# Holding back the last two experts' down weights until the eighth pass's rows have landed

## The chip, the cores and the metric

The kernel runs on one core of one Trainium2 chip. The metric is the device time of one execution in microseconds (us), taken as the median of several runs; smaller is better.

## The reference, cut to what matters

One decoder layer runs over 536 tokens of width 1024: 16 meta tokens, 512 prompt tokens and 8 sample tokens. First comes a mixer (RWKV-7 time mixing and retention, merged by gates, then an output projection). Then comes the part that the change touches, a mixture of 16 experts of which every token uses two, and a final RMSNorm:

```python
x = x + m
x = x + hier_moe(rmsnorm(x, p['norm2_g']), p)
...
h = (jax.nn.silu(jnp.einsum('btd,edf->btef', u, p['expert_w_gate']))
     * jnp.einsum('btd,edf->btef', u, p['expert_w_up']))
h = h * combine[..., None].astype(h.dtype)
return jnp.einsum('btef,efd->btd', h, p['expert_w_down'])
...
y_prompt = rmsnorm(xp[:, N_META:], final_norm_g)
```

All in float32. `combine` is zero except at a token's two experts (top 2 of 4 within the best of 4 groups). A gate and up weight of one expert is 2 MB together (`w_gu`), its down weight 1 MB (`w_dn`).

## The kernel before, in words

The mixer fills the first 640 us and is not touched. After it, the residual rows `x2` lie in DRAM (`x2_dram`, shown as x_rows) and the normed rows in another DRAM tensor (u_rows). Every expert has 96 slots for tokens (`CAP`), so 16 experts make 1536 slots, worked through as 12 passes of 128 slots (`NPASS`), numbered 0 to 11. A pass covers parts of two experts. Slots without a token carry an index out of bounds, and their rows are skipped by the indirect DMAs.

For a pass `e` the work goes round all engines:

- GpSimd (POOL) gathers its 128 rows from u_rows (L1069).
- TensorE (PE) transposes them (`to_channels`, L2589), multiplies them by the gate and up weights (`gate_up`, L2609), transposes the hidden rows (`hidden_in`, L2618) and multiplies them by the down weights (`down`, L2643; for the last pass L2636).
- ScalarE (ACT) does the sigmoid (L2678), copies the transposed hidden rows (`hidden_out`, L2684), and for passes 0 to 7 scales the product rows (`rows_out`, L2693).
- VectorE (DVE) forms the gated product and scales the transposed inputs (L2765).
- For passes 0 to 7 POOL then scatters the rows onto `x2_dram` with an add in the DMA (L2551). Each such scatter raises the semaphore `q_yd[e % 2]` by 16. `ADDS` holds the full counts: 80 for the even passes 0, 2, 4, 6, 8, and 64 for the odd passes 1, 3, 5, 7. So `q_yd[1]` is at 64 once the scatter of pass 7, the eighth, has landed.
- Pass 8 (`SUMS`) is different: its residual rows are gathered ahead (L2557), DVE adds the product to them (L2819), and POOL scatters the sums without an add (L2546).
- Passes 9, 10 and 11 (the three `LATE` ones) never go back to `x2_dram`. When all scatters have landed, POOL gathers their residual rows (L2564), DVE adds their products (L2811, and L2844 in two halves for pass 11), and the rows are normed and scattered straight into the output (L2576).

The order on TensorE near the end is: gate_up(9), down(8), to_channels(11), gate_up(10), hidden_in(9), gate_up(11), hidden_in(10), down(9), hidden_in(11), down(10), down(11).

The final norm of the other tokens runs on tiles of 128 rows, 0 to 4. When both `q_yd` semaphores are full (L2510), SyncE (SP) loads the five tiles from `x2_dram` into SBUF (L2515). ACT squares and sums a tile (L2706) and takes the root (L2715), DVE takes the reciprocal (L2803) and multiplies (L2805), and SP stores the tile (L2520). ACT's instruction stream interleaves these with the last passes: tiles 0 and 1 are squared before the sigmoid and the hidden copy that passes 10 and 11 need, tile 2 after them. So the first two tiles gate the last passes too.

The weights: SP issues all weight loads into six buffers (`NWE`), in one queue, in the order of the loop at L2503. In step `i` it waits until the buffer's gate and up part is free and issues `load_gu(i)` (L957), then waits until the down part of buffer `i - 1` is free and issues `load_dn(i - 1)` (L960). The experts are numbered 0 to 15 in order of use; `load_dn(14)` is issued in step 15 and `load_dn(15)` in step 16. `load_gu(15)` comes before `load_dn(14)`. `down(10)` is the first to use down weight 14 and `down(11)` the first to use down weight 15.

Of the kernel before, what the change touches and what calls it, by code (L numbers as in the profile page):

```python
# [39 lines left out]
NE, NG, EPG, FF = 16, 4, 4, 256  # L40
# [21 lines left out]
def expert_at(i):  # L62

    return EPG * (i % NG) + i // NG
# [379 lines left out]
def hybrid_step(nc, I, O):  # L444

    with ExitStack() as ctx:
# [3 lines left out]
        def sem(name):  # L450
            assert name not in sem_names
            sem_names.add(name)
            return E(nc.semaphore(name))
# [320 lines left out]
        def un_ps(kind, n):  # L774
            p0, p1, c0, c1 = UNITS[n]
            return job_ps((kind, n), (p1 - p0) * (c1 - c0)).rearrange("t (p k) -> t p k", p=p1 - p0)

        NLEV = [sum(1 for b in LEVELS[1:] if b < w) for _, w in CHUNKS]

        def tiles_of(c):  # L780
# [149 lines left out]
        q_yd = [sem(f"q_yd{i}") for i in range(2)]  # L930
# [19 lines left out]
        def rows_of(t):  # L950
            return LASTT if t == TT - 1 else P
# [4 lines left out]
        def load_gu(eng, i):  # L956
            eng.dma_start(we[i % NWE][:, 0:4096], I["w_gu"][expert_at(i)]).then_inc(s_we[i % NWE], 16)  # L957

        def load_dn(eng, i):
            eng.dma_start(we[i % NWE][:, 4096:6144], I["w_dn"][expert_at(i)]).then_inc(s_wd[i % NWE], 16)  # L960

        def load_expert(eng, i):
            load_gu(eng, i)
            load_dn(eng, i)
# [316 lines left out]
        def _(pe):  # L1281
# [8 lines left out]
            def first_pair(step, part):  # L1290

                _, m, hf = step
                ps = job_ps(step) if part else open_job(step)
                i = (m - RET0) // RH
                edges = FIRST[(m, hf)]
                if hf == 0 and part == 0:
                    pe.wait_ge(s_w[i], 16)
                for k in range(edges[part], edges[part + 1]):
                    if (m, hf, k) == (RET0, 0, KD // 2):
                        pe.wait_ge(s_rets, 16)  # L1300
                    if i == 0:
                        pe.wait_ge(s_xg, KD * hf + k + 1)
                    last = mm(ps, wt[:, i, k, :], xg[:, k, cols(hf)], start=(k == 0), stop=(k == KD - 1))  # L1303
                if part == len(edges) - 2:
                    last.then_inc(s_job, 1)

            def whole(step, part):

                _, m, hf = step
                ps = job_ps(step) if part else open_job(step)  # L1310
                side = FILL[0].index(m)
                if part == 0:
                    pe.wait_ge(s_w[2], 32)
                for k in range(2 * part, 2 * part + 2):
                    last = mm(ps, fill_in(0)[side][:, k // 2, k % 2, :], u[:, k, cols(hf)], start=(k == 0), stop=(k == KD - 1))  # L1315
                if part == PARTS["j_proj"] - 1:
                    last.then_inc(s_job, 1)
# [1130 lines left out]
        ADDS = [16 * len(range(q, NPASS - LATE, 2)) for q in range(2)]  # L2448
# [13 lines left out]
        def last_pass(i):  # L2462
            return (CAP * (i + 1) - 1) // P
# [22 lines left out]
        with nc.Fori(0, rounds) as r:  # L2486
            def at_least(eng, s, per, n):
                assert n > 0
                eng.wait_ge(s, r * per + n)

            with nc.Block(no_gpsimd_drain=True) as block:
                @block.sync
                def _(sp):
                    sp.wait_ge(d_x, 3)
                    sp.wait_ge(d_lt, 3)
                    for q in range(2):
                        at_least(sp, q_g[q], EVERY, 16)
                    load_dn(sp, 3)
                    sp.dma_start(O["retp"], ret_st).then_inc(z_out[1], 16)
                    load_expert(sp, 4)  # L2500
                    sp.wait_ge(d_x2w, 16 * TT)
                    load_expert(sp, 5)
                    for i in range(NWE, NE + 1):  # L2503
                        if i < NE:
                            at_least(sp, q_gu, NPASS, last_pass(i - NWE) + 1)
                            load_gu(sp, i)
                        if i > NWE:
                            at_least(sp, q_dn, DOWNS, last_pass(i - 1 - NWE) + 1)
                            load_dn(sp, i - 1)
                    for q in range(2):  # L2510
                        at_least(sp, q_yd[q], ADDS[q], ADDS[q])
                        sp.nop(nofuse=True)
                    for t in range(TT):
                        n = rows_of(t)
                        sp.dma_start(xf[0:n, t, :], x2_dram[t * P:t * P + n, :]).then_inc(z_x[t], 16)  # L2515
                    for t in range(TT):
                        at_least(sp, z_y, TT + LATE, t + 1)
                        sp.nop(nofuse=True)
                        n = rows_of(t)
                        sp.dma_start(O["y"][t * P:t * P + n, :], xf[0:n, t, :]).then_inc(z_out[t % 2], 16)  # L2520
                    for j in range(LATE):
                        at_least(sp, z_late[j], 16, 16)
                    sp.nop(nofuse=True)
                    at_least(sp, z_out[0], 48, 48)
                    at_least(sp, z_out[1], 48, 48)
                    sp.nop(nofuse=True)
# [430 lines left out]
```

## Time and profile before

| | |
|---|---|
| median of 3 runs | 811.1 us (810.11 to 812.12) |
| the profiled execution's own time | 811.99 us |
| its span | 810.5 us |
| PE busy | 778.4 us (96%) |
| DVE, ACT, POOL busy | 432.5, 210.8, 39.2 us |
| bytes moved by DMA | 127.19 MB |
| mean granted TensorE clock | 0.987 of full speed |

The span runs from the first to the last instruction that the profiler recorded. The 1.5 us between it and the profiled execution's time lie around it. Times in the rows below count from the span's start. A DMA instruction's row tells when it was issued and how long the issuing engine was held; when its data landed is a time of its own, given from the start of the issue. A row of the chain names what the end of the program was waiting for at that moment.

### The profile page before, as it was taken

The numbers are of one execution on the slowest core, as the hardware profiler recorded it, in microseconds if no ns is written. First come the engines' busy times: TensorE is split into PE (matmuls) and PEld (weight loads), VectorE is DVE, ScalarE is ACT, GpSimd is POOL, SyncE is SP. The second block draws the span as 40 slices with busy tenths as digits, with TensorE's granted clock in tenths as the row PEclk, the third lists the DMA queues.
The fourth block names the chain that finished last, engine by engine and source line by source line (L and its number), as shares of the span: only waits on it lengthen the run. The fifth ranks groups of instructions, "written<-read, shape, count | busy, mean of one in ns | idle before, by whom it ended". The sixth has DMA issues, their size and how long they took to land.

```text
span 810.5 us, 19993 instructions
## 1 busy us (share of the span) xinstructions
PE 778.4 (96%) x8538; PEld 537.0 (66%) x8538; DVE 432.5 (53%) x855; ACT 210.8 (26%) x497; POOL 39.2 (5%) x50
## 2 busy tenths in 40 slices
PE   7999999999999999999999999999999889999993
PEld 5877777787767877777777877767788633333331
DVE  5965667688768565657666555346204431101135
ACT  4122222254523312211212232220022411111134
POOL 0000000000000000000000000000000011222111
PEclk9999999999999999999999999999999889999997
DMA  9541432432212101201230112064935689999964
GB/s 328 194 157 52 134 106 77 159 105 73 83 53 80 53 28 56 68 15 52 74 121 28 34 50 80 3 234 197 357 131 199 240 304 401 392 404 387 379 225 164
DMA packets 36678, 127.19 MB, mean 157 GB/s; under 512 B 5827, under 2 KB 16099, under 8 KB 31728
## 3 DMA queue, kind: packets, MB, share of 16 engines
q1 hardware_dynamic: 32560, 115.78, 38.3%
q0 software_dynamic: 4032, 10.15, 4.2%
q8 instruction: 68, 1.11, 0.6%
q14 instruction: 18, 0.15, 0.1%
HBM read 106.83 MB, written 18.68 MB: 155 GB/s over the span
## 4 chain that ended last, share of the span: by engine, by line
PE 89%; DVE 5%; DMA 3%; issue 2%; ACT 1%; SPq 0%; POOL 0%; DVEq 0%; POOLq 0%; ACTq 0%
PE psum L1370 23%; PE psum L1351 12%; PE psum L1703 9%; PE psum L2609 9%; PE psum L2643 4%; PE psum L1328 4%; DVE arena L2050 2%; PE psum L1315 2%; PE psum L1303 2%; PE psum L1571 2%; PE psum L1659 1%; PE psum L1584 1%; PE psum L2589 1%; PE psum L1468 1%; PE psum L1480 1%
## 5 line engine op out<-in xcount | busy, mean ns | idle before, releaser
L2050 DVE TENSOR_TENSOR arena<-arena 128x268 f32<-128x268 f32 (+10 forms) x322 | 175.3, 544 | 48.0 <-ACT arena L1802 28.8
L1370 PE MATMUL psum<-arena 128*128 128x268 f32 x784 | 189.5, 393 | 0.0
L1370 PEld LDWEIGHTS psum<-arena 128*128 128x128 f32 x784 | 145.1, 189 | 37.8 <-issue 11.6
L1802 ACT ACTIVATE arena<-psum 128x268 f32<-128x268 f32 (+7 forms) x215 | 85.5, 405 | 276.9 <-PE psum L1370 143.9
L2050 DVE TENSOR_TENSOR arena<-psum,arena 128x256 f32<-128x256 f32 (+5 forms) x170 | 71.7, 426 | 80.2 <-PE psum L1584 21.8
L1351 PE MATMUL psum<-arena 128*128 128x268 f32 x392 | 105.0, 402 | 0.0
L1703 PE MATMUL psum<-arena 128*128 128x268 f32 x384 | 91.0, 391 | 1.6 <-DVE arena L2050 1.2
L2609 PE MATMUL psum<-arena 128*32 128x512 f32 (+1 forms) x640 | 85.7, 597 | 0.5 <-DVE arena L2765 0.3
L1351 PEld LDWEIGHTS psum<-arena 128*128 128x128 f32 x392 | 69.7, 189 | 20.4 <-issue 6.3
L1703 PEld LDWEIGHTS psum<-arena 128*128 128x128 f32 x384 | 71.1, 189 | 17.7 <-issue 3.3
L2765 DVE TENSOR_TENSOR arena<-psum,arena 128x256 f32<-128x256 f32 (+2 forms) x38 | 24.3, 663 | 100.7 <-ACT arena L2678 90.8
L1802 ACT ACTIVATE arena<-arena 128x268 f32<-128x268 f32 (+10 forms) x121 | 49.4, 454 | 105.6 <-PE psum L1715 59.0
L2609 PEld LDWEIGHTS psum<-arena 128*32 128x32 f32 (+1 forms) x640 | 25.2, 115 | 57.4 <-issue 56.8
L2053 DVE SCALAR_TENSOR_TENSOR arena<-arena 128x536 f32<-128x536 f32 (+7 forms) x71 | 41.6, 585 | 12.7 <-DMA arena<-arena 5.8
L2643 PE MATMUL psum<-arena 128*32 128x512 f32 (+1 forms) x288 | 40.2, 596 | 0.0
L2053 DVE SCALAR_TENSOR_TENSOR arena<-psum,arena 128x268 f32<-128x268 f32 (+2 forms) x23 | 10.3, 450 | 47.7 <-PE psum L1703 39.6
L1328 PE MATMUL psum<-arena 128*128 128x268 f32 x128 | 34.4, 401 | 0.0
L2053 DVE SCALAR_TENSOR_TENSOR arena<-arena,psum 128x268 f32<-128x268 f32 (+1 forms) x36 | 18.8, 522 | 19.7 <-PE psum L1703 12.2
L1274 POOL MEMSET arena<- 64x256 f32 (+1 forms) x18 | 5.5, 312 | 489.9 <-PE psum L1370 266.2
L2050 DVE TENSOR_TENSOR arena<-arena,psum 128x268 f32<-128x268 f32 (+3 forms) x35 | 18.2, 520 | 18.8 <-PE psum L1351 14.2
L1328 PEld LDWEIGHTS psum<-arena 128*128 128x128 f32 x128 | 22.7, 189 | 6.5 <-issue 1.9
L2643 PEld LDWEIGHTS psum<-arena 128*32 128x32 f32 (+1 forms) x288 | 10.8, 115 | 21.3 <-issue 21.3
(210 smaller groups left out, 696.0 us busy)
## 6 DMA issues: line engine op xcount, KB each, us to landing
arena<-in_w_gu SPq DMA_DIRECT2D x16, 2048.0 KB, 21.7
arena<-in_w_in SPq DMA_DIRECT2D x45, 512.0 KB, 4.4
arena<-in_w_dn SPq DMA_DIRECT2D x16, 1024.0 KB, 20.0
arena<-in_w_out SPq DMA_DIRECT2D x2, 2048.0 KB, 14.1
arena<-arena SPq DMA_DIRECT2D x5, 536.0 KB, 5.9
arena<-in_x SPq DMA_DIRECT2D x8, 268.0 KB, 5.5
arena<-arena SPq DMA_DIRECT2D x16, 134.0 KB, 4.5
arena<-in_x SPq DMA_DIRECT2D x1, 2144.0 KB, 14.5
```

The costliest lines, as they stand in the source:

```text
L1303: last = mm(ps, wt[:, i, k, :], xg[:, k, cols(hf)], start=(k == 0), stop=(k == KD - 1))
L1315: last = mm(ps, fill_in(0)[side][:, k // 2, k % 2, :], u[:, k, cols(hf)], start=(k == 0), stop=(k == KD - 1))
L1328: last = mm(ps, bb_tile(m)[:, k, :], ret_o[:, k, cols(hf)], start=(k == 0), stop=(k == NP - 1))
L1351: last = mm(ps, w[:, k // 2, k % 2, :], x[:, k, :], start=(k == 0 and i in (0, 1, 3)), stop=(k == KD // 2 - 1), skip_group_check=i not in ...
L1370: last = mm(ps, w[:, k, :], x[:, k, :], start=(k == 0 and i in (0, 1, 3)), stop=(k == KD // 2 - 1), skip_group_check=i not in (0, 1, 3))
L1703: last = mm(ps, w[:, k, :], x[:, k, cols(hf)], start=(k == 0), stop=(k == nk - 1))
L1802: run(nc.scalar.activation(out, in_, fn, **kw), s)
L2050: run(v.tensor_tensor(out, a, b, op), s)
L2053: run(v.scalar_tensor_tensor(out, a, sc_, b, op0, op1), s)
L2609: last = mm(bank(2 + i % 2)[part], ue[:, i % 2, k, part], w_gu[x % NWE][:, k, :], start=(k == 0), stop=(k == KD - 1))
L2643: last = mm(bank(down_bank(e) + q)[part], hht(e)[:, f, part], w_dn[x % NWE][:, f, 512 * q:512 * q + 512], start=(f == 0), stop=(f == 1))
L2765: v.tensor_tensor(out, x, y, op).then_inc(s, 1)
```

## The change

SyncE gets one more wait, ahead of the issue of down weight 14. With NE = 16 the condition holds in step 15 only. Down weight 15, the next instruction but one in the same stream, thereby also comes after it.

```diff
@@ -2506,6 +2506,8 @@
                             load_gu(sp, i)
                         if i > NWE:
                             at_least(sp, q_dn, DOWNS, last_pass(i - 1 - NWE) + 1)
+                            if i - 1 == NE - 2:
+                                at_least(sp, q_yd[1], ADDS[1], ADDS[1])
                             load_dn(sp, i - 1)
                     for q in range(2):
                         at_least(sp, q_yd[q], ADDS[q], ADDS[q])
```

## Rows read from the trace of the kernel before

**Rows 1.** The page: shares of the chain that ended last, by engine.
```profile
PE 89%; DVE 5%; DMA 3%; issue 2%; ACT 1%; SPq 0%; POOL 0%; DVEq 0%; POOLq 0%; ACTq 0%
```

**Rows 2.** The chain that ended last, 764 to 811: start us, us, what.
```profile
766.33 3.62 PE psum L2643 x32
769.97 1.30 DVE arena L2819
...
772.10 7.71 DMA x_rows<-arena,ids
...
780.00 4.47 DMA arena<-x_rows
...
793.71 1.28 DVE arena L2811
```

**Rows 3.** Instructions in order of time on SP: start, us, line; x2 is two.
```profile
741.56 0.33 SPq L957 DMA_DIRECT2D arena<-in_w_gu  x1
746.40 12.02 SPq L960 DMA_DIRECT2D arena<-in_w_dn  x2
...
758.10 0.33 SPq L960 DMA_DIRECT2D arena<-in_w_dn  x1
```

**Rows 4.** Instructions in order of time on POOL, in brackets the idle time before.
```profile
760.14 1.60 POOL L2551 DMA_INDIRECT x_rows<-arena,ids  x1 [3.86 <-ACT arena L2693]
772.10 1.00 POOL L2546 DMA_INDIRECT x_rows<-arena,ids  x1 [10.37 <-DVE arena L2819]
780.76 1.03 POOL L2564 DMA_INDIRECT arena<-x_rows,ids  x1 [7.66 <-DMA x_rows<-arena,ids]
```

**Rows 5.** DMA issues one at a time, from 741.56, 746.40, 758.10, 760.14: us to landing last.
```profile
arena<-in_w_gu SPq DMA_DIRECT2D x1, 2048.0 KB, 32.2
...
arena<-in_w_dn SPq DMA_DIRECT2D x1, 1024.0 KB, 30.1
...
arena<-in_w_dn SPq DMA_DIRECT2D x1, 1024.0 KB, 21.5
...
x_rows<-arena,ids POOLq DMA_INDIRECT x1, 15.0
```

**Rows 6.** DMA issues: output scatters; all down-weight loads; third tile load; last late gather.
```profile
out_y<-arena,ids POOLq DMA_INDIRECT x3, 3.3
...
DMA to landing us min/median/max: 4.8/20.0/30.9
...
arena<-x_rows SPq DMA_DIRECT2D x1, 512.0 KB, 7.4
...
arena<-x_rows,ids POOLq DMA_INDIRECT x1, 8.4
```

**Rows 7.** Busy time by stretch; the last two columns are DMA share and GB/s.
```profile
764.00:768.00 4.00, 4.00 (x39) 1.77 (x34) 2.00 (x3) 0.73 (x2) 0.00 (x0) 1.00 1.01 381
768.00:772.00 4.00, 3.66 (x32) 1.59 (x26) 1.91 (x2) 0.00 (x0) 0.00 (x0) 1.00 0.78 255
772.00:776.00 4.00, 4.00 (x20) 1.29 (x18) 0.60 (x1) 0.00 (x0) 1.00 (x1) 1.00 0.41 156
776.00:780.00 4.00, 4.00 (x29) 1.21 (x29) 0.85 (x2) 1.57 (x3) 0.00 (x0) 1.00 0.13 55
```

**Rows 8.** DMA queues from 782 to 785: packets, MB, share of 16 engines.
```profile
q1 hardware_dynamic: 265, 0.96, 81.3%
q0 software_dynamic: 84, 0.21, 22.3%
```

**Rows 9.** Instructions in order of time on PE and ACT, 770 to 796.
```profile
770.25 1.09 PE L2589 MATMUL psum<-arena 128*128 128x128 f32 x8 [0.34 <-DMA arena<-u_rows,ids]
...
790.47 3.66 PE L2643 MATMUL psum<-arena 128*64 128x512 f32 x16
795.13 3.64 PE L2636 MATMUL psum<-arena 128*32 128x512 f32 x32 [1.00 <-DVE arena L2811]
...
784.49 1.06 ACT L2706 ACTIVATE arena<-arena 128x1024 f32<-128x1024 f32 x1 [3.82 <-DMA arena<-x_rows]
...
785.87 1.04 ACT L2706 ACTIVATE arena<-arena 128x1024 f32<-128x1024 f32 x1
```

## The prediction

> **What bounds the kernel now.** I read the page first, then the chain of waits from 764 us on, then the DMA issues one by one, and last the DMA share by stretch. The page says that the chain is 89% TensorE [rows 1], and up to 770 us there is nothing for this change to shorten: the chain is matmuls back to back. At the end it is different. From 769.97 the chain goes through L2819 on VectorE, then through the last scatter (772.10, 7.71 us), then through the load of row tile 0 (issued 780.00, 4.47 us), and from there through ScalarE and VectorE to the end [rows 2]. TensorE has idle time in this part (1.00 us ahead of the last pass's down product [rows 9]), so 12.2 us of pure DMA time stand on the path. If these get shorter or longer, the end moves with them.
>
> Why does the scatter of pass 8 take 7.71 us, when the output scatters at the very end land 3.3 us after their issue [rows 6]? Look at what is in flight. Gate/up weight 15 was issued at 741.56 and took 32.2 us, so it landed at 773.8. Down weight 14, issued at 746.40, took 30.1 and landed at 776.5. Down weight 15, issued at 758.10, took 21.5 and landed at 779.6 [rows 3, 5]. The three come in the order of issue, and the last comes 0.2 us before the scatter (779.8). The scatter of pass 7, issued at 760.14, took 15.0 us and landed at 775.1 [rows 4, 5]. In the same stretches the DMA share falls from 1.01 to 0.78, 0.41 and 0.13 [rows 7]: most of the 16 DMA engines have drained, and a few still work off all of their queue. Skipped rows explain that (my reading): slots without a token are always the last ones of an expert's 96, so some engines get more real rows than others. A transfer has landed only when the last engine has done its part, so the laggards set all these times.
>
> **The change, part by part.**
>
> Issue. Down weight 14 moves from 746.40 to the landing of the scatter of pass 7, and down weight 15 from 758.10 to right after it. Behind the waiting SyncE instruction stand down weight 15, the wait for both scatter semaphores, the five tile loads and the stores. Gate/up weight 15 is ahead of it. The wait is not met already: 746.40 against 775.1. One more wait instruction costs nothing to see, SyncE is idle there.
>
> Landing of the scatter of pass 7. The laggards' queue up to gate/up weight 15 is as before, for the down weights stood behind it. The gathered input of pass 11 landed at 770.25 (TensorE waited 0.34 us for it [rows 9]) and is ahead of the scatter in POOL's queue, so the scatter used 4.9 us from 770.2 to 775.1. Up to 773.8 all is as before, 3.6 of the 4.9 us. The other 1.3 us ran beside down weight 14. POOL's queue has 22% of the engines' time when both queues are full [rows 8], so alone the rest takes 0.3 us: 774.1. One more gain is possible: while all engines are busy, each moves 381 / (16 x 1.01) = 23.6 GB/s, in the drained stretch 55 / (16 x 0.13) = 26 [rows 7]. With 2 MB fewer on the other engines the laggards could gain up to 10% over some 7 us, 0.7 us. I take a small part of it: 773.9. Bounds: 773.3 and 775.1 (no gain).
>
> Landing of the scatter of pass 8. Its issue, 772.10, hangs on TensorE and VectorE and stays. It now follows pass 7's on empty queues: 3.3 us from issue would be 775.4, but its data start only at 773.9, some 2.3 us more give 776.3; I take 776.5. Bounds 775.4 and 779.8. So the tile loads are issued at 776.7 and not at 780.00, and the late gathers at 777.4 and not at 780.76 [rows 4]. This is the gain, 3.3 us at the issue.
>
> What it triggers. The tile loads stand in SyncE's queue behind 2.1 MB of down weights that are only now on their way. The shortest landing of one down weight was 4.8 us [rows 6]; the second adds 1.05 MB at 0.39 MB per us (0.96 + 0.21 MB in 3 us [rows 8]), 2.7 us. Issued at 774.1, the pair is in at 781.6 if nothing else runs. From about 778.5 the three late gathers take 22%, 0.6 us more: 782.2. Then tile 0: 0.52 MB at 78% of 0.39 is 1.7 us, so 783.9, against 784.47 before. Tile 1 comes 1.7 us later, at 785.6; ScalarE squared it at 785.87 before [rows 9]. So of 3.3 us about 0.3 are left, and the chain behind ScalarE starts 0.3 us earlier. The 2.1 MB were moved from a time when the DMA engines ran anyway into the hole (share 0.41 and 0.13) ahead of the tile loads, and they fill that hole to the brim.
>
> Covers. Down weight 14 is first used at 790.47, down weight 15 at 795.13 [rows 9]. At 779 and 782 they have 11 and 13 us; only landing later than that would cost. Tile 2 landed 7.4 us after its issue at 780.85 (788.2) and the last late gather 8.4 after 783.41 (791.8) [rows 6]; VectorE used it at 793.71 [rows 2]. The same bytes after a shorter pause end no later: from 775 on, 2.1 MB of down weights, 2.2 of tiles and 1.1 of gathers (about 90 rows of 4 KB each) are 5.4 MB or 13.8 us, 789.
>
> **The sum.** 811.99 for the profiled execution, minus 0.3, is 811.7. That execution stood 0.9 above the median of the runs shown, so on the median 811.1 - 0.3 = 810.8. The case's own range: from 809.6 to 812.0, by the bounds of the scatter of pass 7 (-0.6 and +1.2 on the tile loads).
>
> **A rule of the Trainium skill that speaks against this.** In the stretch from 782 to 785 POOL's queue moved 0.21 MB beside 0.96 MB of SyncE's [rows 8], though its first gather started late in it. The Trainium skill, "DMA: Bandwidth & Descriptors", section "Queues, rings and completion order", says that each DMA engine goes in turn between the queues that have work, a packet at a time. Equal turns of packets of equal bytes would give the late gathers half, not 22%; what that would give is the second rival. The row speaks for less than half, but not clearly.
>
> **Rivals.**
>
> 1. The gain gets through, 809.1. The scatter of pass 7 lands at 773.3 and the down weights pass before the late gathers take much: the pair lands at 781.0, tile 0 at 782.5 and tile 1 at 783.9. ScalarE's chain starts 2.0 us earlier. For it: the 10% faster engines above, and a hole of 8 us for 5.4 us of transfer. Against it: it needs the late gathers to cost nothing beside the pair.
>
> 2. Slower, 812.7. The late gathers take half of the engines from 778.9, since they are issued early now. Then some 0.8 MB of down weights, tile 0 (0.52) and up to 1.1 MB of gathers must pass first: 2.4 / 0.39 = 6.2 us, 785.1, and 1 us to the landing, 786.1. Tile 1 follows at 787.4 against 785.87: about +1.6. This decides as soon as gathers are issued while more than half a megabyte of down weights is still out. For it: the tiles are last in their queue, and the path hangs on the first two. Against it: the 22%.
>
> 3. The change does not do what it says for the scatter, 811.6. Its semaphore comes at 775.1 as before, and the down weights (data from 776) meet pass 8's scatter on all engines. It lands near 779.8, the tile loads find the tail of the pair ahead: tile 0 at 785.0, +0.5.
>
> 4. A new stall of TensorE for a down weight, or anything larger than these: beyond 2.4 us either way.
>
> **How the numbers follow.** Forecast 0.50, rival 1 0.20, rival 2 0.14, rival 3 0.09, rival 4 0.07. 0.3% is 2.4 us, and less than that a measurement of this kernel cannot tell from no change. Forecast, rivals 2 and 3 lie inside it; rival 1 at -2.0 with its spread falls outside in about four of ten, 0.08. With 0.05 and 0.02 of rival 4: faster 0.13, same 0.80, slower 0.07. The range of 808.6 to 813.0 takes in rivals 1 and 2 with their spread.
>
> **What the changed profile would show.** SyncE's two L960 issues side by side near 774, the first after a wait for DMA on x_rows. The scatter of pass 8 in the chain at about 4.4 us and not 7.71. The load of tile 0 issued near 776.7 and taking about 7 us and not 4.47: the gain turned into queueing. DMA share near 1 from 776 on. TensorE at L2643 and L2636 without a wait for weights. The prediction is wrong if tile 0's load starts early and stays at 4 to 5 us (rival 1 or more), if the late gathers land long before tile 0 (rival 2), or if the issues stand later than 775.1.

## The result

The changed kernel is slower. Its median was 813.62 us (812.08 to 815.43, 8 runs) beside 811.89 for the kernel before on the same chip (8 runs). The ratio, which the comparison gives and which is a little off the quotient of the two medians, is 1.0026, 95% interval 1.0016 to 1.0036, so +1.3 to +2.9 us. The forecast was 810.8 (0.3 us faster) and a range of 808.6 to 813.0. The profiled execution took 812.84 us with a span of 811.3.

The changed kernel's line numbers are two higher from the change on. Its chain of waits from 760 on (start us, us, what) answers to [rows 2]:

```profile
766.54 3.62 PE psum L2645 x32
770.19 1.30 DVE arena L2821
...
772.32 3.25 DMA x_rows<-arena,ids
...
776.08 10.48 DMA arena<-x_rows
...
794.44 1.28 DVE arena L2813
```

The scatter of pass 8 takes 3.25 us and not 7.71. But the load behind it now takes 10.48 us and is tile 1's (it ends at 786.56); before it was tile 0's, 4.47 us. The two DMA steps together went from 12.2 to 13.7 us.

The instructions on SP and on POOL, in order of time, answer to [rows 3, 4]:

```profile
741.78 0.33 SPq L957 DMA_DIRECT2D arena<-in_w_gu  x1
773.71 0.96 SPq L960 DMA_DIRECT2D arena<-in_w_dn  x2
775.71 2.44 SPq L2517 DMA_DIRECT2D arena<-x_rows  x5
```

```profile
760.36 1.60 POOL L2553 DMA_INDIRECT x_rows<-arena,ids  x1 [3.86 <-ACT arena L2695]
772.32 1.00 POOL L2548 DMA_INDIRECT x_rows<-arena,ids  x1 [10.37 <-DVE arena L2821]
776.53 1.03 POOL L2566 DMA_INDIRECT arena<-x_rows,ids  x1 [3.21 <-DMA x_rows<-arena,ids]
```

Both down weights leave from 773.7 on, the tiles 4.3 us and the late gathers 4.2 us earlier than before. How long the scatters of passes 7 and 8 took to land, from the DMA issues (before: 15.0 [rows 5] and 7.71):

```profile
x_rows<-arena,ids POOLq DMA_INDIRECT x1, 13.3
...
x_rows<-arena,ids POOLq DMA_INDIRECT x1, 3.3
```

Busy time by stretch (last columns DMA share and GB/s) answers to [rows 7]. The DMA engines are partly idle from 764 to 776 and then full up to 788:

```profile
764.00:768.00 4.00, 4.00 (x40) 1.77 (x34) 2.00 (x3) 0.73 (x2) 0.00 (x0) 1.00 0.69 210
768.00:772.00 4.00, 4.00 (x33) 1.61 (x27) 1.81 (x2) 0.00 (x0) 0.00 (x0) 1.00 0.23 73
772.00:776.00 4.00, 4.00 (x22) 1.41 (x20) 0.61 (x1) 0.00 (x0) 1.00 (x1) 1.00 0.50 151
776.00:780.00 4.00, 4.00 (x30) 1.19 (x30) 0.85 (x2) 1.75 (x3) 2.86 (x3) 1.00 1.00 408
780.00:784.00 4.00, 4.00 (x40) 1.18 (x36) 0.00 (x0) 0.48 (x2) 0.17 (x1) 1.00 1.02 414
784.00:788.00 4.00, 4.00 (x38) 1.14 (x34) 1.46 (x2) 2.83 (x6) 0.00 (x0) 1.00 1.00 389
```

The two DMA queues of the changed kernel, from 778 to 781 and from 781 to 784 (packets, MB, share of 16 engines):

```profile
q1 hardware_dynamic: 187, 1.18, 94.0%
q0 software_dynamic: 13, 0.04, 3.1%
...
q1 hardware_dynamic: 189, 0.70, 57.5%
q0 software_dynamic: 188, 0.55, 45.4%
```

The upper of each pair is SyncE's queue, the lower POOL's. POOL's queue, the late gathers, has 45% in the second stretch; the forecast used 22% from [rows 8]. What ScalarE and TensorE make of it, beside [rows 9]:

```profile
784.48 1.06 ACT L2708 ACTIVATE arena<-arena 128x1024 f32<-128x1024 f32 x1 [3.99 <-DMA arena<-x_rows]
786.58 1.06 ACT L2708 ACTIVATE arena<-arena 128x1024 f32<-128x1024 f32 x1 [0.63 <-DMA arena<-x_rows]
```

```profile
785.50 0.44 PE L2620 MATMUL psum<-arena 128*128 128x128 f32 x2
790.82 0.44 PE L2620 MATMUL psum<-arena 128*128 128x128 f32 x2 [1.30 <-DVE arena L2767]
795.86 3.64 PE L2638 MATMUL psum<-arena 128*32 128x512 f32 x32 [1.01 <-DVE arena L2813]
```

ScalarE waits for tile 0 as before and then 0.63 us more for tile 1; TensorE's last stretch waits for what comes of that, and never for a weight. All behind it is 0.7 us later.

**A measure for the tail.** What lies ahead of this stretch shifts by up to 4 us from one profile to the next (the product below ends between 785.49 and 789.51), so profiles are compared here from the end of pass 11's gate/up product (the first PE row above, 785.50) to the end of the span. This tail was 810.5 - 785.69 = 24.8 us in the first profile of before and 25.8 in the changed kernel.

### The profile page after: what moved, and what is told of

It is laid out like the page before. It is cut to its first block, busy times and chain, and to the rows that moved or that the text cites. A ratio compares the mean times of both kernels' runs of the same rounds, so it can differ in the third digit from the quotient of the medians.

```text
span 811.3 us, 19993 instructions
## 1 busy us (share of the span) xinstructions
PE 778.5 (96%) x8538; PEld 536.7 (66%) x8538; DVE 432.4 (53%) x855; ACT 211.1 (26%) x497; POOL 39.2 (5%) x50
## 4 chain that ended last, share of the span: by engine, by line
PE 89%; DVE 5%; DMA 3%; issue 2%; ACT 1%; SPq 0%; POOL 0%; DVEq 0%; POOLq 0%; ACTq 0%
PE psum L1370 23%; PE psum L1351 12%; PE psum L1703 9%; PE psum L2611 9%; PE psum L2645 4%; PE psum L1328 4%; DVE arena L2050 2%; PE psum L1315 2%; PE psum L1303 2%; PE psum L1571 2%; PE psum L1659 1%; PE psum L1584 1%; DMA arena<-x_rows 1%; PE psum L2591 1%; PE psum L1468 1%
## 5 line engine op out<-in xcount | busy, mean ns | idle before, releaser
L2053 DVE SCALAR_TENSOR_TENSOR arena<-arena,psum 128x268 f32<-128x268 f32 (+1 forms) x36 | 18.8, 521 | 19.8 <-PE psum L1703 12.2
```

Of the source, the lines that this page charges most:

```text
L2053: run(v.scalar_tensor_tensor(out, a, sc_, b, op0, op1), s)
```

## The experiments

Each edit is against the kernel before unless it says otherwise. Ratios are to the kernel before on the same chip. "The tail" is the measure above, from one profile each.

**Cut down weights, with the wait.** Nearly all of down weights 14 and 15 is left out of the transfers. Edit on the changed kernel:

```diff
+            n = 6144 if i < NE - 2 else 4224
-            eng.dma_start(we[i % NWE][:, 4096:6144], I["w_dn"][expert_at(i)]).then_inc(s_wd[i % NWE], 16)
+            eng.dma_start(we[i % NWE][:, 4096:n], I["w_dn"][expert_at(i)][:, 0:n - 4096]).then_inc(s_wd[i % NWE], 16)
```

> The changed kernel, but the last two experts' down weights load only 64 of their 2048 columns (their products are then wrong); wait and order stay. Theory A (the 2.1 MB ahead of the row tiles in SyncE's queue give the scatter's gain back): the scatter of pass 8 lands 3.3 us after its issue as in the changed kernel, tile 0 lands 4.5 us after its issue near 780.2 and not at 784.5, tile 1 by 781.6, and the time falls to about 2.5 us under the kernel before (ratio 0.997), where TensorE's gate/up product of pass 11 (end near 785.6) takes over as the bound. Theory B (the wait or the late issue itself costs, or TensorE lacks the weights): tile 0 stays near 784 and the time stays 1 to 2 us over the kernel before.

Measured: 809.72 us, ratio 0.9968 (0.9955 to 0.9980), tail 808.6 - 786.62 = 22.0 us. ScalarE's first square no longer waits for a tile, and TensorE's last product waits for nothing. ScalarE, then TensorE:

```profile
781.52 1.05 ACT L2709 ACTIVATE arena<-arena 128x1024 f32<-128x1024 f32 x1
```

```profile
794.53 3.64 PE L2639 MATMUL psum<-arena 128*32 128x512 f32 x32
```

So theory A holds: with the wait in place and the bytes gone, the loss is gone, and the bytes ahead of the tiles are the cost.

**The same cut without the wait.**

> The kernel before (no extra wait), with the last two experts' down weights cut to 64 of their 2048 columns (their products are then wrong). Theory A (the wait itself costs nothing, only where the 2.1 MB stand): the same time as the run with the cut weights and the wait, 2.4 us under the kernel before (ratio 0.997), the scatter of pass 8 landing 3.3 to 3.5 us after its issue. Rival (the wait or the late issue has a cost of its own): 0.5 us or more faster than that run.

Measured: 809.69 us, ratio 0.9967 (0.9955 to 0.9980), tail 811.5 - 789.51 = 22.0 us. The same, within intervals of some 1 us either way: no cost of the wait itself can be seen, and the pair of down weights costs the kernel before 2.7 us, the changed kernel 4.8 (1.0026 - 0.9967 of 812 us).

**Only the last down weight held.** Edit on the changed kernel (down weight 14 leaves as in the kernel before):

```diff
-                            if i - 1 == NE - 2:
+                            if i - 1 == NE - 1:
```

> Only down weight 15 is held for the scatter of pass 7; down weight 14 is issued at 746.4 as before. Theory A: 1.05 MB instead of 2.1 MB stand ahead of the tiles, but the lagging DMA engines still carry down weight 14 to 776.5. The scatter of pass 7 lands at 775.1, down weight 15 is in at about 780, the scatter of pass 8 near 777.5, tile 0 lands near 783 and tile 1 near 785: the time is 0.5 to 1 us under the kernel before. Theory B (holding any weight costs in itself): between the kernel before and the changed one, about +0.9 us.

Measured: 810.86 us, ratio 0.9986 (0.9978 to 0.9995), faster than both kernels; tail 24.1. The squares of tiles 0 and 1:

```profile
782.35 1.06 ACT L2708 ACTIVATE arena<-arena 128x1024 f32<-128x1024 f32 x1 [1.61 <-DMA arena<-x_rows]
...
785.09 1.06 ACT L2708 ACTIVATE arena<-arena 128x1024 f32<-128x1024 f32 x1 [1.26 <-DMA arena<-x_rows]
```

**The same once more.**

> Down weight 15 alone held for the scatter of pass 7, once more: 1 to 1.3 us under the kernel before (ratio 0.998 to 0.999), tile 1 in ScalarE 0.4 to 0.8 us before the end of TensorE's gate/up product of pass 11. Rival (the first time was chance): ratio 1.000.

Measured: 810.75 us, ratio 0.9981 (0.9972 to 0.9990), tail 23.5. ScalarE started on tile 1 at 784.81, 1.7 us ahead of the end of gate/up (786.51), more than the 0.4 to 0.8 expected. The scatter of pass 8 took 5.73 us here and 3.85 in the run before. The chain ends over the last late gather (issued 781.71, 11.39 us), for which VectorE waits 0.47 us, and no longer over a tile.

**Late gathers held back, in the changed kernel.** POOL waits for tile 0 ahead of them:

```diff
+                    then(z_x[0], 16, 16)
                     for j in range(LATE):
                         e = FIRST_LATE + j
                         pool.indirect_dma_start(late[:, j, :], None, x2_dram,
```

> The changed kernel, and POOL issues the three late gathers only when tile 0 has landed. Theory A with the gathers' share as the term that was too small: tiles 0 and 1 land about 1.1 and 1.5 us earlier than in the changed kernel, at 783.4 and 785.1, tile 1 before ScalarE wants it; but the gathers land some 4 us later than in the changed kernel, the last near 792.5, about when VectorE wants it, so that the time is within 0.5 us of the kernel before (1 to 2 us under the changed kernel). Rival (the down weights alone fill the time, the gathers take nothing that matters): tile 0 stays at 784.5, tile 1 at 786.6, and the time is that of the changed kernel or up to 1 us over it.

Measured: 813.08 us, ratio 1.0026 (1.0010 to 1.0041). In the profile tiles 0 and 1 come 2.0 and 1.4 us earlier than in the changed kernel:

```profile
782.49 1.06 ACT L2709 ACTIVATE arena<-arena 128x1024 f32<-128x1024 f32 x1 [1.92 <-DMA arena<-x_rows]
785.19 1.06 ACT L2709 ACTIVATE arena<-arena 128x1024 f32<-128x1024 f32 x1 [1.23 <-DMA arena<-x_rows]
```

The down weights of this run, issued at 773.9 and 774.6, from the DMA issues:

```profile
arena<-in_w_dn SPq DMA_DIRECT2D x1, 1024.0 KB, 4.8
...
arena<-in_w_dn SPq DMA_DIRECT2D x1, 1024.0 KB, 6.8
```

The pair was in at 781.4, 7.5 us after its issue, which is what the forecast gave it when alone. So the gathers do delay the tiles. The time was not better, though: the chain of this run ends over the last gather (786.67, 5.86 us, just when VectorE wants it), the profiled execution (811.43) was among the fastest of its 12, and they reached to 817.84. In this profile the gathers' cost was moved and not removed. The expected time (within 0.5 us of the kernel before) did not come, and what makes this kernel's times spread over 6.7 us was not profiled.

**The same in the kernel before.**

> The kernel before (no wait for the weights), and POOL issues the late gathers only when tile 0 has landed. Theory A: with no down weights in front, tile 0 stays near 784.5 and tile 1 was in time already, so nothing is won there, and the last gather lands 3 to 4 us later than before (near 795 and not 791.8), after VectorE wants it at 793.7: 1 to 2.5 us slower than the kernel before. Rival (gathers cost the tiles much here too, and their own landing does not matter): faster by 0.5 us or more.

Measured: 813.3 us, ratio 1.0019 (1.0010 to 1.0028): slower by 1.5 us, as theory A has it. Its profile shows this only in part, for it is that of the fastest of the 12 executions (811.67). The last gather (787.03, 5.90 us) lands at 792.9 and not near 795, and again VectorE adds right behind it. Tile 0 was squared at 782.85 and not near 784.5.

**Tiles 0 and 1 ahead of both down weights.**

```diff
+                            if i - 1 >= NE - 2:
+                                continue
...
                         sp.dma_start(xf[0:n, t, :], x2_dram[t * P:t * P + n, :]).then_inc(z_x[t], 16)
+                        if t == 1:
+                            for x in range(NE - 2, NE):
+                                load_dn(sp, x)
```

> No extra wait: SyncE issues row tiles 0 and 1 as soon as all scatters have landed, then down weights 14 and 15, then tiles 2 to 4. Theory A (what costs is the order in SyncE's queue): the scatter of pass 8 lands at 775.6, tile 0 near 780.2, tile 1 near 781.8, ScalarE waits for TensorE's pass 11 (785.6) and no longer for tiles; down weight 14 lands near 786, before its use at 790; tile 2 near 789. The time is 1.5 to 2.5 us under the kernel before. Theory B (the weights come too late for TensorE when they are issued this late): a wait of TensorE for a down weight of over 1 us, and the time over that of the kernel before.

Measured: 813.29 us, ratio 1.0010 (1.0000 to 1.0020), tail 26.3. Tiles 0 and 1 came as expected (ScalarE squared them at 780.39 and 781.76), but tile 2 came at 792.06 and not 789:

```profile
792.06 1.06 ACT L2711 ACTIVATE arena<-arena 128x1024 f32<-128x1024 f32 x1 [4.18 <-DMA arena<-x_rows]
```

TensorE waits 2.91 us ahead of its last product, but for VectorE and not for a weight, so theory B's stall is not there:

```profile
796.39 5.34 PE L2641 MATMUL psum<-arena 128*32 128x512 f32 x32 [2.91 <-DVE arena L2816]
```

The product took 5.34 us and not 3.64: behind the idle stretch the mean granted clock was 0.72 from 796 to 798 and 0.50, the lower of its two levels (1.2 GHz), from 798 to 800. The chain of this run goes over VectorE there, so this cost nothing that the profile shows. The expectation in time was wrong. In both orders the pair ahead of the next tile that ScalarE needs stands on the path.

**Last down weight behind tiles 0 and 1** (`NE - 1` for `NE - 2` in both places of the last edit):

> Down weight 14 is issued at 746.4 as in the kernel before; down weight 15 behind tiles 0 and 1 and ahead of tiles 2 to 4. Theory A: the scatter of pass 8 lands near 776.4, tiles 0 and 1 near 781 and 782.5, and 1 MB less than in the run with both weights behind tiles 0 and 1 stands ahead of tile 2: it lands near 789.5 and not at 792.0, just before or after ScalarE wants it (788.5 to 789): 1 to 2 us under the kernel before. Rival (TensorE lacks down weight 15, or tile 2 is as late as there): no gain.

Measured: 811.83 us, ratio 0.9998 (0.9988 to 1.0008): no gain that can be told, where 1 to 2 us were expected. In the profile the tail is 22.6 and VectorE waits for a late gather:

```profile
792.51 1.28 DVE L2816 SCALAR_TENSOR_TENSOR arena<-psum,arena 128x1024 f32<-128x1024 f32 x1 [0.57 <-DMA arena<-x_rows,ids]
```

**Last down weight behind all tiles** (`t == 4` for `t == 1` besides):

> As the run before this one, but down weight 15 is issued behind all five row tiles. Theory A: nothing stands ahead of any tile; tile 2 lands near 786, the last gather near 788 to 789, down weight 15 near 790, before its use at 794. What is left is TensorE's order, so the time is that of the run whose last two down weights were cut to 64 columns, 2 to 2.6 us under the kernel before (ratio 0.997). Rival (the last down weight comes late): TensorE waits ahead of its last down product for the weight, and the time is at or over the kernel before.

Measured: 811.11 us, ratio 0.9994 (0.9985 to 1.0004), where 0.997 was expected. The profile's tail is 22.3 us, as good as expected, and TensorE waits for no weight. Why the median shows less than the profile's tail stays open; one profile each is not enough. The late gather stands right at VectorE's need here too (a wait of 0.18 us), so an execution in which it lands later would lose as much.

**The changed kernel once more.**

> The changed kernel once more, beside the others on one chip. 1.5 to 2 us over the kernel before (ratio 1.002 to 1.003). In its trace tile 0 lands near 784.5 and tile 1 near 786.6, two us apart, with POOL's queue at 40 to 50% of the engines between 781 and 784. If tile 1 lands later here than in the first trace, the time is later by as much (theory A: the end hangs on tile 1); if not, the spread of this kernel has another cause.

Measured: 814.58 us, ratio 1.0028 (1.0019 to 1.0037), tail 813.1 - 786.51 = 26.6. Tile 1 was squared 1.95 us after the end of gate/up, against 1.08 in the first profile, and the tail is longer by as much (0.8). POOL's queue has 33.2% from 781 to 784 and not the 40 to 50% expected, but all is 1 us later here: from 782 to 785 it has 44.5%.

```profile
785.88 1.06 ACT L2708 ACTIVATE arena<-arena 128x1024 f32<-128x1024 f32 x1 [4.38 <-DMA arena<-x_rows]
...
788.46 1.06 ACT L2708 ACTIVATE arena<-arena 128x1024 f32<-128x1024 f32 x1 [1.10 <-DMA arena<-x_rows]
```

**The kernel before once more.**

> The kernel before, unchanged, for a second profile and as a measure of the noise: ratio within 0.999 and 1.001. Theory A, for the part of the slowdown that the first profile of the changed kernel does not show: here ScalarE starts on tile 1 within 0.4 us of the end of TensorE's gate/up product of pass 11, as in the first profile of before (0.2 us after it), against 1.1 and 1.9 us after it in the two profiles of the changed kernel. Rival: it comes 1 us or more after it here too, and the profiles do not tell the two kernels apart.

Measured: 812.03 us, ratio 1.0002 (0.9993 to 1.0012), tail 24.0. Its last scatter, from the DMA issues, and ScalarE's squares of tiles 0 and 1:

```profile
x_rows<-arena,ids POOLq DMA_INDIRECT x1, 6.3
```

```profile
782.63 1.06 ACT L2706 ACTIVATE arena<-arena 128x1024 f32<-128x1024 f32 x1 [1.86 <-DMA arena<-x_rows]
...
784.02 1.05 ACT L2706 ACTIVATE arena<-arena 128x1024 f32<-128x1024 f32 x1
```

Tile 1 was squared 1.8 us before the end of gate/up, where the expectation had it within 0.4 us, and the scatter landed in 6.3 us and not 7.71. So no tile is on the path of this profile. Its chain goes from the scatter over the last late gather, for which VectorE waits:

```profile
782.50 10.41 DMA arena<-x_rows,ids
```

```profile
793.02 1.29 DVE L2811 SCALAR_TENSOR_TENSOR arena<-psum,arena 128x1024 f32<-128x1024 f32 x1 [1.08 <-DMA arena<-x_rows,ids]
```

The kernel before thus has two DMA ends close to each other, tile 1 and the last gather, and either can be the last.

## Why the prediction was wrong

**Right.** That two DMA steps in a row bound the end; in the second profile of before the second step is a late gather and not a tile. The landing of the scatter of pass 7 (773.9 forecast; the weights left at 773.7). The scatter of pass 8 landed at 775.6, 0.9 us before the 776.5 forecast, which won nothing, since the tiles then stood behind the weights. The pair of down weights alone (7.5 us forecast and measured). No wait of TensorE for a weight. That the gain turns into queueing behind 2.1 MB.

**Wrong, the term that was mis-sized.** "From about 778.5 the three late gathers take 22%": the step "What it triggers" gave tile 0 at 783.9 and tile 1 at 785.6, and they were used at 784.48 and 786.58. [Rows 8] average a stretch, 782 to 785, in which POOL's queue moved nothing up to 784. From 784 to 787, with both queues full, the kernel before shows (queues, as above):

```profile
q1 hardware_dynamic: 180, 0.63, 60.8%
q0 software_dynamic: 147, 0.42, 40.7%
```

That row was there to be read. In the changed kernel POOL's queue moved nothing from 778 to 780.7, though all three gathers had been issued by 779.2, and from 780.7 to the landing of tile 1 at 786.56 the queues show:

```profile
q1 hardware_dynamic: 378, 1.40, 58.6%
q0 software_dynamic: 371, 1.00, 43.0%
```

The forecast had the gathers move some 0.6 MB by the landing of tile 1 (22% of 0.39 MB per us over 7.1 us). It was 1.0 MB. At 0.39 MB per us the other 0.4 MB are 1.0 us, and tile 1 was 1.0 us later than forecast. That the two agree so well is partly luck: the weights also left 0.4 us earlier than forecast, and the sum gave the time from a transfer's last byte to its landing nothing. Tile 1 then stood 1.1 us behind the end of gate/up, and the forecast's gain of 0.3 us was a loss of 0.7 in the two first profiles.

This is the mechanism of rival 2, and its side was the right one. Its sizes (half of the engines from 778.9, tile 1 at 787.4) were too large, and that its 812.7 us lies nearest to the measured time is partly luck: in the profile tile 1 moved by 0.7 us and not by its 1.6. The rule of turns by packet, which the prediction cites from the Trainium skill, "DMA: Bandwidth & Descriptors", section "Queues, rings and completion order", agrees with the trace: 378 and 371 packets.

With the gathers held back the tiles came 2.0 and 1.4 us earlier; but tile 1 still came 2.7 us after tile 0 there, where 1.7 were forecast. SyncE's queue had 99% of the engines between the two landings and moved 1.08 MB, twice a tile. So half of it was data of later tiles, which passed before tile 1 was whole; the forecast had one tile follow the other. Why tile 1 was not whole is not settled.

**Wrong, the baseline.** The median of three, 811.1, was 811.89 with eight runs: 0.8 us of the 2.8 between forecast and measured time is this. And the gain was sized by the one profile of before: 7.71 us for the scatter, 4.47 for the load of tile 0, tile 1 squared at 785.87. The second profile had 6.3 us, 3.5 and 784.02. A third, of the kernel in which only the gathers wait, is the same program up to there and had 7.56 us and 3.63. So the first was late in both steps, in the load more clearly than in the scatter. Taking the two profiles of each kernel, the tail is 24.4 us before and 26.2 after, a difference of 1.8 us, which is near the measured 1.7 to 2.4 (the differences of the medians in the two comparisons). With the first profiles alone it is 1.0. Two profiles each are few, and those of before end over different waits; that this is all of it is argued and not shown.

**Two smaller slips.** The "case's own range" goes down to 809.6, but its bound of -0.6 us on the tile loads gives 810.2. And the prediction held that less than 0.3% could not be told from no change: 0.26% and 0.28% were told from it.

**Open.** That skipped rows make some DMA engines lag was not tried. That the down weights are what held the scatter is shown: with them cut to 64 columns it landed in 3.5 us at the latest.

## What to carry to other kernels

A transfer that is held back does not get cheaper: ask what is issued right behind it in the same queue, and hold back only what fits the hole ahead of that (here one weight, 1 MB: ratio 0.9981 to 0.9986) and not twice as much (1.0026 and 1.0028). Where the argument rests on a DMA's landing time, take the queues' shares from a stretch in which both are full, and doubt a gain that is sized by one execution's landing. Look too for a second wait that ends close to the first: where the tiles came early, the last gather bound the end (VectorE waited 0.47 and 1.08 us for it).

## What was not expected of the hardware

The same scatter in the same kernel landed in 7.71 us in one execution and 6.3 in another, behind the same 2.1 MB (7.56 in the kernel in which only the gathers wait). With one weight held it took 3.85 and 5.73. In both profiles of the changed kernel, with none of the 2.1 MB in the queue at its issue, it took 3.3, and in the kernels with cut weights 3.2 and 3.5.

The first late gather's data started only 3 to 4 us after its issue, with SyncE's queue busy (before: issued 780.76, nothing moved up to 784; changed: 776.53 and 780.7). From then on the two queues of the changed kernel took packets in nearly equal number.
